# Another order of four engines around the first sparse scores of a sparse-attention trunk, and small columns stored inside other tensors

## The reference, cut to what matters

```
k_cmp = gelu((blocks(k) + pe) @ w1k + b1k) @ w2k         # 31 compressed keys
v_cmp = gelu((blocks(v) + pe) @ w1v + b1v) @ w2v         # 31 compressed values
o_c = softmax(mask(q @ k_cmp.T)) @ v_cmp                 # compressed branch
o_s = softmax(causal(rope(q) @ rope(ks).T)) @ vs         # selected blocks (all 8 blocks are selected)
o_w = softmax(causal(rope(q) @ rope(kw).T)) @ vw         # window
out = (g0 * o_c + g1 * o_s + g2 * o_w) @ w_o
```

## Time and profile before

| | |
|---|---|
| median of 3 runs | 1358.13 us |
| the profiled execution | 1358.98 us |
| its span in the trace | 1357.2 us |
| mean granted clock of TensorE | 0.994 |
| PE busy | 97% of the span |
| DVE, ACT, POOL busy | 47%, 50%, 45% |

### The profile page before, as it was taken

How to read it: one execution, slowest core, us unless ns; L and a number is a source line. 1 busy time by engine, 2 the same in 40 slices (tenths; PEclk the granted TensorE clock), 3 DMA queues, 4 the chain that set the end, 5 groups by cost and what they waited for, 6 DMA issues and landing times.

```text
span 1357.2 us, 19897 instructions
## 1 busy us (share of the span) xinstructions
PE 1320.9 (97%) x6872; PEld 1109.6 (82%) x6872; DVE 633.8 (47%) x1478; ACT 678.0 (50%) x1261; POOL 604.1 (45%) x401
## 2 busy tenths in 40 slices
PE   9989999989999999999999999998999999999997
PEld 6878888877888888888889788886898888888886
DVE  4357777782644434430015667768354333441005
ACT  4457777774444444441225777776244444443122
POOL 2458686763244444444434222332344444444442
PEclk9989999999999999999999999999999999999999
DMA  9633232224233333334323412312433333334321
GB/s 293 138 86 79 70 79 79 71 55 143 76 93 98 104 93 93 93 93 145 102 79 96 102 48 65 80 64 66 152 94 109 93 104 96 93 100 133 99 72 63
DMA packets 172798, 131.98 MB, mean 97 GB/s; under 512 B 24544, under 2 KB 156244, under 8 KB 172724
## 3 DMA queue, kind: packets, MB, share of 16 engines
q1 hardware_dynamic: 172724, 131.02, 33.4%
HBM read 117.17 MB, written 4.39 MB: 90 GB/s over the span
## 4 chain that ended last, share of the span: by engine, by line
PE 89%; DVE 4%; ACT 3%; issue 2%; POOL 1%; DMA 0%; SPq 0%; DVEq 0%; ACTq 0%; POOLq 0%
PE ps L1007 16%; PE ps L1008 16%; PE ps L1009 16%; PE ps L1275 7%; PE ps L1274 7%; PE ps L1277 7%; PE ps L1162 3%; PE ps L1134 2%; PE ps L1176 2%; PE ps L1326 2%; PE ps L1322 2%; PE ps L1321 2%; PE ps L1175 1%; PE ps L1086 1%; PE ps L1265 1%
## 5 line engine op out<-in xcount | busy, mean ns | idle before, releaser
L512 POOL TENSOR_TENSOR wl<-raw,wh 128x1024 fp32r<-128x1024 f32 x178 | 427.1, 2403 | 646.6 <-ACT wh L639 646.5
L1007 PE MATMUL ps<-xh,wh 128*128 128x512 f32 x960 | 378.9, 395 | 5.0 <-ACT qf L714 3.6
L1008 PE MATMUL ps<-xl,wh 128*128 128x512 f32 x960 | 375.6, 391 | 0.0
L1009 PE MATMUL ps<-xh,wl 128*128 128x512 f32 x960 | 375.3, 391 | 0.0
L639 ACT ACTIVATE wh<-raw 128x1024 fp32r<-128x1024 f32 x192 | 201.1, 1050 | 198.2 <-PE ps L1277 184.6
L1007 PEld LDWEIGHTS ps<-xh,wh 128*128 128x128 f32 x960 | 181.1, 189 | 42.1 <-ACT qf L714 4.5
L1009 PEld LDWEIGHTS ps<-xh,wl 128*128 128x128 f32 x960 | 181.0, 189 | 38.6
L1008 PEld LDWEIGHTS ps<-xl,wh 128*128 128x128 f32 x960 | 181.1, 189 | 33.1
L1794 DVE SCALAR_TENSOR_TENSOR work<-ps,conv,work 128x511 f32<-128x511 f32 x88 | 66.0, 749 | 222.0 <-ACT work L874 156.1
L734 ACT ACTIVATE prob<-prob,negmax 128x128 f32<-128x128 f32 x192 | 107.4, 559 | 56.2 <-DVE negmax L1559 54.0
L1275 PE MATMUL ps<-wl,gh 128*128 128x512 f32 x344 | 135.2, 393 | 0.0
(11 more groups left out here) (233 smaller groups left out, 1970.3 us busy)
## 6 DMA issues: line engine op xcount, KB each, us to landing
raw<-in_ffn_w_up SPq DMA_DIRECT2D x88, 512.0 KB, 3.8
raw<-in_ffn_w_down SPq DMA_DIRECT2D x44, 512.0 KB, 3.5
raw<-in_fox_w_in SPq DMA_DIRECT2D x24, 512.0 KB, 4.1
raw<-in_nsa_w_in SPq DMA_DIRECT2D x12, 512.0 KB, 5.0
xt<-in_x SPq DMA_DIRECT2D x8, 512.0 KB, 5.0
raw<-in_nsa_w_in SPq DMA_DIRECT2D x16, 256.0 KB, 3.7
qs<-work SPq DMA_DIRECT2D x32, 128.0 KB, 2.3
raw<-in_nsa_w_o SPq DMA_DIRECT2D x8, 512.0 KB, 3.6
```

Of the source, the lines that this page charges most:

```text
L512: nc.gpsimd.tensor_tensor(wl[:, slot, :, :], raw[:, slot, :, :], wh[:, slot, :, :].bitcast(F32), ALU.subtract).then_inc(s_wl, 1)
L1007: nc.tensor.matmul(o, ah, bh, start=start, stop=False)
L1008: nc.tensor.matmul(o, ah, bl, start=False, stop=False)
L1009: return nc.tensor.matmul(o, al, bh, start=False, stop=stop)
```

## The change

**Small columns.** Six tensors of one or two columns of 4 bytes each (`zero`, `last_mean`, `half_gap`, `first_var`, `last_var`, `second_squares`) become columns of `eps_zero`, `negmean` and `squares`. Each tensor takes 32 bytes of a partition at least, and tensors lie one behind the other in the order of the code, so all that is allocated behind them starts 192 bytes earlier: `table`, `warm`, `prob`, `pth`, `ptl`, `xt`, `oh`, `ol`, `gh`, `gl`, `qs`, `ks`, `kw`, `vv`, `qf` and the others of the overlays. `xh`, `xl`, `raw`, `wh`, `wl` and `work` stay. By the sizes in the code the moved ones began 64 bytes past a multiple of 128 bytes and now begin at one, as the unmoved ones do.

**Order.** The instructions of the attention are the same but for one: a load of the Exp table ahead of its need (`load_table(ACT.Exp)`, a 128x1 activation). What moves:

- PE: `cmp_scores(0)` and the scores of units 0 and 1 come straight after chunk 6; the values' transposes, the convolution's constants and the compressed values' last product (which now goes to bank 7, the constants to bank 5) come after them. The wait for `conv_copy(1)` moves from the scores of unit 0 to the turn of unit 1, and a wait for `vcs` stands ahead of its first use.
- DVE: the maxima of units 0 and 1 come right after `cmp_mask(0)`; `vcs`'s low part (4 instructions) goes behind the turns u = 3 and 4, the values' low part and the compressed sum, inverse, gate and scale behind the maximum of unit 2.
- ACT: the table load comes ahead of `item_hi(0, 1)`; the exponentials of units 0 and 1 ahead of `cmp_exp(0)`; chunk 9's high part and `vcs`'s high part go into the turns u = 0, 1 and 2.
- POOL: chunk 9's low part, one instruction before, becomes three, behind the scales of units 2, 3 and 4.

```diff
-            for c in range(7, 10):
+            for c in range(7, 9):
                 lo(c, c % R)
...
+                    if u in (1, 2, 3):
+                        lo_part(9, 3 * (u - 1), min(3 * u, KB))
...
             cmp_gelu(1)
+            load_table(ACT.Exp)
             item_hi(0, 1)
             item_copy(0, 2)
-            act.wait_ge(s_cmpo, 2)
-            for n in range(4):
-                last = nc.scalar.activation(vcs[n * CS:n * CS + NCMP, 0, n % 2, :, :],
-                                            ps[0:NCMP, 4, 0:GROUPS * HD].rearrange("p (g d) -> p g d", g=GROUPS), ACT.Copy)
-            last.then_inc(s_vh, 1)
+            unit_exp(0, 0)
+            unit_exp(1, 1)
+            cmp_exp(0)
             item_hi(0, 2)
-            cmp_exp(0)
-            hi(9, 9 % R)
...
                     unit_hi(u, w % 4)
+                    if u == 0:
+                        hi(9, 9 % R)
+                    if u in (1, 2):
+                        cmp_values_hi(range(2 * (u - 1), 2 * u))
...
             def turn(u, i):
                 pe.wait_ge(s_pr, u + 1)
+                if u == 1:
+                    pe.wait_ge(s_vc, 4)
...
                 if p % 4 == 1:
+                    if p == 1:
+                        pe.wait_ge(s_cmpr, 2)
...
             item_steps(2)
+            pe.wait_ge(s_cmpr, 1)
+            cmp_scores(0)
+            pe.wait_ge(s_ge, 4)
+            nsa_scores(0)
+            nsa_scores(1)
+            values_turn(0, BO)
+            conv_turn(1, BT + 1)
             pe.wait_ge(s_gel, 2)
...
-            pe.wait_ge(s_cmpr, 1)
-            cmp_scores(0)
-            values_turn(0, BO)
-            conv_turn(1)
-
-            pe.wait_ge(s_vc, 4)
-            pe.wait_ge(s_ge, 4)
-            nsa_scores(0)
-            nsa_scores(1)
```

More of the change, by code:

```diff
@@ L111, in build_trunk @@
         zsum = sb("zsum", [P, QT, 2])
-        negmean = sb("negmean", [P, QT])
-        squares = sb("squares", [P, QT])
+        negmean = sb("negmean", [P, QT + 2])
+        last_mean = negmean[:, QT:QT + 2]
+        squares = sb("squares", [P, QT + 4])
+        half_gap, first_var, last_var, second_squares = [squares[:, c:c + 1] for c in range(QT, QT + 4)]
         std = sb("std", [P, QT])
         rstd = sb("rstd", [P, QT])
-        zero = sb("zero", [P, 1])
-        last_mean = sb("last_mean", [P, 2])
-        half_gap = sb("half_gap", [P, 1])
-        first_var = sb("first_var", [P, 1])
-        last_var = sb("last_var", [P, 1])
-        second_squares = sb("second_squares", [P, 1])
         table = sb("table", [P, 1])
@@ L756, in heads_hi, with load_table, cmp_values_hi @@
                 nc.scalar.activation(o[:, n % KB, :], head_sum, ACT.Copy).then_inc(s_oh, 1)
+            def load_table(func):
+                nc.scalar.activation(table[:, :], eps[:, :], func)
+            def cmp_values_hi(ns):
+                act.wait_ge(s_cmpo, 2)
+                for n in ns:
+                    nc.scalar.activation(vcs[n * CS:n * CS + NCMP, 0, n % 2, :, :],
+                                         ps[0:NCMP, BO + 1, 0:GROUPS * HD].rearrange("p (g d) -> p g d", g=GROUPS), ACT.Copy).then_inc(s_vh, 1)
             def cmp_exp(H):
@@ L781, in _ @@
                     n = u // 8 + 3
-                    for x in ([0, 1, 2] if u == 0 else [v + 2]):
-                        uu = 32 * g + x
-                        if uu < NSA_UNITS:
-                            unit_exp(uu, uu % 4)
+                    if u + 2 < NSA_UNITS:
+                        unit_exp(u + 2, (u + 2) % 4)
                     if w == 6 and u // 8 % 2 and u + 2 < NSA_UNITS:
@@ L810, in _ @@
             heads_hi(KB - 1, oh)
-            def load_table(func):
-                nc.scalar.activation(table[:, :], eps[:, :], func)
             def tile_std(n, m):
@@ L1216, in _ @@
                 for hb in range(2):
-                    last = nc.tensor.matmul(ps[0:NCMP, 4, g * HD:(g + 1) * HD], ghid[:, hb, g * NCMP:(g + 1) * NCMP], w2v[:, hb, :],
+                    last = nc.tensor.matmul(ps[0:NCMP, BO + 1, g * HD:(g + 1) * HD], ghid[:, hb, g * NCMP:(g + 1) * NCMP], w2v[:, hb, :],
                                             start=(hb == 0), stop=(hb == 1))
             last.then_inc(s_cmpo, 1)
-            pe.wait_ge(s_cmpr, 1)
-            cmp_scores(0)
-            values_turn(0, BO)
-            conv_turn(1)
-            pe.wait_ge(s_vc, 4)
-            pe.wait_ge(s_ge, 4)
-            nsa_scores(0)
-            nsa_scores(1)
             for g in range(GROUPS):
@@ L1522, in _, with conv_copy @@
             cmp_blocks(1)
[L1524 removed]
+            def conv_copy(l, bank):
                 dve.wait_ge(s_vt, 6 + 4 * l)
[L1526 to L1528 removed]
+                nc.vector.tensor_copy(conv[:, l, :, :], ps[:, bank, :].rearrange("p (w c) -> p w c", w=4)[:, :, 0:2 * FB]).then_inc(s_vc, 1)
+            conv_copy(0, BO + 1)
             dve.wait_ge(s_ld[10], 32)
@@ L1633, in _, with cmp_values_lo @@
                 item_dve(0, k)
-            cmp_mask(0)
-            cmp_difference(0)
-            dve.wait_ge(s_vh, 1)
-            for n in range(4):
-                last = nc.vector.tensor_tensor(vcs[n * CS:n * CS + NCMP, 1, n % 2, :, :],
-                                               ps[0:NCMP, 4, 0:GROUPS * HD].rearrange("p (g d) -> p g d", g=GROUPS),
-                                               vcs[n * CS:n * CS + NCMP, 0, n % 2, :, :].bitcast(F32), ALU.subtract)
-            last.then_inc(s_cmpr, 1)
-            item_dve(0, 2)
-            conv_copy(1)
-            for step in (cmp_sum, cmp_inverse, cmp_gate, cmp_scale):
-                step(0)
+            def cmp_values_lo(ns):
+                dve.wait_ge(s_vh, 4)
+                for n in ns:
+                    last = nc.vector.tensor_tensor(vcs[n * CS:n * CS + NCMP, 1, n % 2, :, :],
+                                                   ps[0:NCMP, BO + 1, 0:GROUPS * HD].rearrange("p (g d) -> p g d", g=GROUPS),
+                                                   vcs[n * CS:n * CS + NCMP, 0, n % 2, :, :].bitcast(F32), ALU.subtract)
+                    if n == 3:
+                        last.then_inc(s_cmpr, 1)
+            cmp_mask(0)
             unit_max(0, 0)
@@ L1648, in _ @@
             unit_inverse(0)
+            cmp_difference(0)
+            conv_copy(1, BT + 1)
             for g in range(GROUPS):
@@ L1663, in _ @@
                         item_dve(*divmod(n - 1, 4))
-                    if v == 0 and g:
+                    if v == 0:
                         item_dve(g, 2)
+                    if u == 0:
+                        cmp_sum(0)
+                        cmp_inverse(0)
+                        cmp_gate(0)
+                    if u in (3, 4):
+                        cmp_values_lo(range(2 * (u - 3), 2 * (u - 2)))
                     if w == 4 and following:
@@ L1674, in _ @@
                         cmp_gate(j)
-                    if u % 16 == 0 and u:
+                    if u % 16 == 0:
                         cmp_scale(u // 16)
```

12 lines of the change are left out of this document (5 added, 7 removed).

## The result

The changed kernel takes 1351.82 us (median of 6 runs, 1349.32 to 1353.09), the kernel before 1358.50 (6 runs, 1357.21 to 1361.37) on the same chip. The ratio is 0.9941 [0.9928, 0.9954], which is 8.0 us less by the ratio (6.2 to 9.8). The forecast was 5.9 us less. By the ratio the time is 1350.1, 0.6 us under the low end of the range.

A forecast was written before the change was run, and what follows sets the result against it. PE, 97% busy, was taken as the bound, losing time to waits and a halved clock in the first stage. A 5.9 us lead at chunk 8, buffers 0, gave 1357.2 - 5.9 = 1351.3 of span, 1352.2 median; range 1350.7 to 1355.2.

The forecast's parts named there:

- `item_hi(0, 1)` starts: First stage, ACT: the queries' high part starts at 69.3 us in place of 68.26, behind the table load.
- last moves issued from: First stage, queries' last two moves: issued from 71.3 us in place of 70.28, shifted by 1.05 with POOL's `rope_lo`.
- scores of unit 0: First stage, PE: they start at 74.25 us, once the queries' moves land, with 0.75 us of idle PE ahead.
- first matmul of unit 1's weight step: First stage, PE: at 79.25 us, 6.8 us ahead of before, with the 2.16 us wait gone.
- first matmul of chunk 8: First stage, PE: at 89.4 us in place of 95.36, after a new wait that loses 0.85 us of the lead.
- lead at chunk 8: PE at the first matmul of chunk 8: 5.9 us ahead of the kernel before, kept to the end.
- The clock did not fall: Rival, first stage: PE's clock falls as before and 2.2 us go, giving 1354.4; chance 0.10.
- DVE and ACT fell behind: Rival, before chunk 8: DVE's 10 us of work take 20% more and 2 us go, giving 1354.2; chance 0.12.
- the table load has no tail: Rival, queries' path on ACT: a tail of 1.28 us behind the load delays unit 0 to 75.5, giving 1353.5; chance 0.06.
- The lead was kept: Rival, after the changed stage: something not moving with PE ends last; 0 to 2.7 us remain, about 1357; chance 0.05.
- The moved buffers: Term for tensors at new addresses: taken as 0, bounded at 1 us either way, from weight loads of 188 and 189 ns.
- the rival on the moved buffers: Rival: instructions on tensors at the new addresses take 3% longer, costing 10 us, giving 1362.7; chance 0.04.

The follow-up runs named there:

- e2: The changed kernel with 192 bytes of padding ahead of `table`, so the old addresses return and only the order is new; 1352.35 us, ratio 0.9955 to before.
- e1_fold_only: The kernel before with only the small columns folded, so the later tensors start 192 bytes earlier; 1357.47 us, ratio 0.9991 to before.
- e8: The changed kernel with a pad of 64 bytes ahead of `table`; 1358.85 us in a single run, the kernel before 1359.28 on its chip.
- e9_pad32: The changed kernel with a pad of 32 bytes ahead of `table`; 1358.45 us in a single run, the kernel before 1361.49 on its chip.
- e10_pad128: The changed kernel with a pad of 128 bytes ahead of `table`; 1358.61 us in a single run, the kernel before 1361.49 on its chip.
- e3: The changed kernel run again without an edit (the repetition); 1351.77 us, ratio 0.9954 to the kernel before.

## Why the prediction was off

Its steps in the changed stage held, each within 0.3 us, once the later start of 0.68 is taken off:

| step | predicted | measured, less 0.68 |
|---|---|---|
| `item_hi(0, 1)` starts | 69.3 | 69.25 |
| last moves issued from | 71.3 | 71.26 |
| scores of unit 0 | 74.25 | 74.39 |
| first matmul of unit 1's weight step | 79.25 | 79.25 |
| first matmul of chunk 8 | 89.4 | 89.70 |
| clock, 75 to 90 us | 1.00 | 1.00 |
| lead at chunk 8 | 5.9 | 5.66 |

The chain that was predicted for chunk 8 is the one that came: DVE's maximum of unit 7 releases ACT at 89.03, 88.35 less the start, where 88.0 was forecast, and from ACT's exponential to PE it is 1.35 us (forecast 1.34). The rivals are decided too. The clock did not fall; DVE and ACT fell behind by 0.3 us, not by 2; and the table load has no tail: of the Trainium skill's page "ScalarE: Activation LUTs", section "What ACT_TABLE_LOAD costs", the load agrees (1.28 us) and the drain of about 1380 ns isn't there. The lead was kept but for scatter: the changed kernel has 4.98 us at 113 us and 5.03 at 305, e2 5.08 and 4.05, and from there e2 holds it to 925 us (4.04). Its 6.04 at the end contain the 2.0 of the race at 936.

The step that failed is "The moved buffers": "1 ns on some 1000 such loads is 1 us, either way; I take 0". The term measured 2.1 us in the trace of `e1_fold_only`, faster (2.0 in the two down projections; 0.4 in each output projection stand against what e1 loses elsewhere). In the times it doesn't stand out from the scatter. What misled was the row that it leaned on: weight loads of `gh` and `wh` take 188 and 189 ns, and so they do afterwards. The sign stood in the matmul rows of the same page, which weren't compared: L1275 has a mean of 393 ns and L1274 one of 391. That they can be 389 to 390 only the trace of the changed kernel tells. The prediction compared how long the loads take, and the cost was in how far apart the matmuls start. A sum of 5.66 + 2.1 = 7.8 us gives 1350.4, which the measured ratios (8.0 and 6.2 us less) surround. The repetition's 6.2 is nearer to the forecast of 5.9 than to this sum, so the times alone wouldn't convict the term; the spacings of the matmuls do. Even the rival on the moved buffers had the wrong frame: it asked whether the new addresses were slower than the old, from a multiple of 128, and not how two tensors stand to each other. With a pad of 32 to 128 bytes the same edit ends at 1357 us of span, and the gain of the order is gone: e8, which has the race and the clock of before at 936 and 760 us, loses 6.1 us from 113 us to the end. The rival that went against the change was real, with a price of some 8 us between best and worst. That this fold landed on the good side is luck as far as the forecast goes, which had no reason for it.

The rest of the profiled 9.7 us is no effect of the change: 2.05 from the race at 936 us, 1.6 - 1.1 from the clock, less 0.7 for the start: 5.66 + 2.1 + 2.05 + 0.5 - 0.7 = 9.6. Such steps are as large as the 2.5 us by which this execution lay under the median of its kernel.

Open: which tensor of which pair it is (none was moved alone); why the clock falls behind one gap and not behind its twin; why the times show less of the fold than the traces; and whether the 47 ns by which DVE has to be ahead hold at any other place.

## What to carry to other kernels

When an engine waits first for work that it needs later, put the work that it has already ahead of that wait, and count the gain as wait plus clock, less the waits that come up next; that sum was right to 0.3 us. An edit that only moves allocations is not free: compare the mean and the spacing of the same large matmul over stages with different operands, and if they differ by 1 or 2%, shift one tensor against the other by 32 to 192 bytes and measure. Measure every pair, since what helps one can hurt another. Where a long GpSimd instruction runs beside short VectorE ones on SBUF, try it in parts; that gained 4.2 us here. Before crediting a profiled difference to an edit, lay the twins of PE's matmuls side by side, and strike the steps that come and go between executions of one program.

## What the runs showed of the hardware

- In these kernels a matmul's rate depends on how the tensors that PE reads stand to each other in SBUF. In the 128x512 products of the down projections the matmuls are 226.5 to 227.1 ns apart at a distance of a multiple of 256 bytes, up to 235.9 at 64, 234.9 at 32, 232.8 at 128 and 231.5 at 192: up to 4%. The Trainium skill, page "SBUF — State Buffer", section "SBUF: two separate sides", says that PE waits for no one at SBUF. With the other engines idle the spacing is the same, so these runs don't speak against that; they show PE slowed without anyone else.
- A multiple of 256 is not the best for every pair. Matmuls of `pcs` with `vcs` (64 columns of weights) are 230.4 ns apart before and 238.1 after; in `e9_pad32`, where these two stand at a multiple of 256, they are 233.4 apart, and 231.0 in `e10_pad128`. It is 16 pairs in each only.
- DVE's scale with both operands in SBUF and POOL's subtraction exclude each other for a whole instruction (0.29 us or 2.50 for 128x128). At the one place where both start nearly together, DVE is held up when it is 30 to 47 ns ahead of POOL by the profile's times, and free at 47 to 60; cutting POOL's 2.4 us instruction in three gave 12.8 us of DVE's time back and some 4 us of the kernel's.
- Two waits of PE close together, 1.7 to 2.1 us in sum, are followed in some executions by 3.4 us at a granted clock of 0.50 (1.2 GHz), which cost 1.3 to 1.6 us, and in others not: near 313 us in after, but not in e3, which is the same program.
